# Router products taken in front of the norm, rows turned inside the output projection, one weight block requested earlier

## The chip, the cores and the metric

The kernel runs on one core of a Trainium2 chip. The time is that of the device for one execution, in microseconds (us); lower is better. The core has TensorE (PE, matrix products into PSUM), VectorE (DVE), ScalarE (ACT), GpSimd (POOL), SyncE (SP, which issues most transfers here) and 16 DMA engines.

## The reference

One decoder layer on 576 tokens (a prompt of 512 and 8 sequences of 8), 1024 wide: a mixer, then hierarchical mixture of experts.

```python
def _layer(x, ...):
    m, new_pool, new_conv = _mixer(x, ...)            # h = x @ w_in, pooling and short convolution, @ w_out
    x = _layer_norm(DEEPNORM_ALPHA * x + m, ln1_g, ln1_b)
    f = _hier_moe(x, w_group, b_group, w_expert, b_expert, w1, w3, w2)
    x = _layer_norm(DEEPNORM_ALPHA * x + f, ln2_g, ln2_b)

def _hier_moe(x, ...):
    g_logits = xf @ w_group + b_group                 # 4 groups, the best one is taken
    e_logits = xf @ w_expert + b_expert               # 8 experts in each, the best two of the group
    ...
    for e in range(N_EXPERTS):                        # 32 experts, 1024 -> 512 -> 1024
        hdn = jax.nn.silu(xf @ w1[e]) * (xf @ w3[e])
        acc = acc + combine[:, e:e + 1] * (hdn @ w2[e])
```

`_layer_norm` subtracts the row's mean, divides by the root of its variance plus 1e-5, multiplies by g and adds b.

## The kernel before, in words

Tokens are in five tiles, four of 128 rows and one of 64 (`ROWS`). The kernel has these stages:

1. Input projection. `project(c)` for 16 parts of w_in, each in three products of high and low parts (fp32r), 48 matrix products a part; pooling maps and the convolution run on DVE and ACT beside it.
2. Output projection. `out_project(h, j)` for the two halves h of the 1024 columns and the tiles j, 24 products each, from `mix_high`, `mix_low` and `wout_part`. In its second half DVE adds the residual, takes mean and variance (`deviation_of`), and normalises the row in place in `x_tok` (`norm1`). When a tile is normalised (`x1_ready`), PE turns it (`turn_x1`: eight transposes), ACT copies it to `x1T` and stores the rows to `x1_rows` in DRAM, and `route` multiplies the turned rows by the router's 36 columns. These pieces stand between the tiles' projections, one or two tiles behind.
3. Choice. DVE adds the bias (`keep_logits`), chooses group and experts in a chain of dependent small operations (`choose`), and PE counts positions from the mask. `keep_warm(n)` is n products of the identity with itself, whose results nobody reads.
4. Fetch. `fetch_first` picks the rows of the first expert tile out of `x_tok` with a one-hot product; `turn_first` turns them. The second tile's rows come by an indirect DMA from `x1_rows` (POOL) and are turned by `turn_second`.
5. Experts. 33 tiles of 64 slots; each has w1, w3 and w2, 2 MB each, streamed through ten blocks of SBUF (`EARLY_BLOCKS`). SP issues the loads in the fixed order of `LOADS`: w1 and w3 of tile 0, of tile 1, w2 of tile 0, and so on. One of the odd pairs after the first, seven in all, has its rows picked by PE (`pick_pair`), the others come by DMA. Load n from the eleventh on waits until the block that it replaces has been used (`block_free`). There are 96 loads.

The first ten blocks share their memory with the stages before, so each has its own condition: load 9 after the first value weights, loads 1 and 2 after the input projection, 5 after the mixer's tails are stored, 6 and 7 after the first half of the output projection, and 0, 3, 4 and 8 after the second half (`out_done` at 10). `mix_high` lies across blocks 3 and 4.

All engines run in order, each its own queue; semaphores join them.

## Time and profile before

| | us |
|---|---|
| three timed runs, median (lowest to highest) | 699.1 (696.45 to 699.15) |
| the profiled execution, its own time | 694.83 |
| its span | 693.1 |
| PE busy in it | 649.9 (94%) |
| DVE busy | 316.2 (46%) |
| ACT busy | 226.1 (33%) |
| POOL busy | 151.5 (22%) |

The mean granted clock was 0.992 of full speed. The span runs from the first to the last instruction; the execution's own time has 1.7 us more. Busy shares are means over stages with different limits, so what a change is worth is read from the stage in which it acts, and from what waits there last.

### The profile page before, as it was taken

To read this page: it belongs to the slowest core of one execution; us is meant where nothing else is said; L and a number is where in the kernel's file an instruction comes from. 1 tells how busy PE (TensorE), PEld (TensorE's weight loads), DVE (VectorE), ACT (ScalarE), POOL (GpSimd) and SP (SyncE) were. 2 spreads that over 40 slices of the span, in tenths; PEclk is the share of its full clock that TensorE was granted. 3 is DMA by queue.
4 is the path that set the end of the run, shared out by engine and by line. 5 is a ranking of instruction groups with operands and counts; after the bars stand their busy time and mean duration, and the time that the engine had idled before them with its cause. 6 is when DMAs were issued, how large, how long until landed. Compare 5 with 4: busy or idle time off the path is not lost.

```text
span 693.1 us, 10915 instructions
## 1 busy us (share of the span) xinstructions
PE 649.9 (94%) x4334; PEld 424.7 (61%) x4334; DVE 316.2 (46%) x829; ACT 226.1 (33%) x330; POOL 151.5 (22%) x180
## 2 busy tenths in 40 slices
PE   5999999999989999999999999999999799789883
PEld 5899999878866555554555555455454454445451
DVE  3562485716676416155154345335433425332555
ACT  3423313301122323344344145253344233413331
POOL 1000000000001214233233323313413223231433
PEclk9999999999999999999999999999999999999998
DMA  9892231836296999999999999999999999999991
GB/s 259 268 320 74 80 122 35 335 133 258 72 425 274 361 389 417 421 417 420 417 418 414 418 417 420 421 422 419 419 419 421 417 418 420 418 421 417 421 402 60
DMA packets 44781, 233.89 MB, mean 337 GB/s; under 512 B 13231, under 2 KB 17839, under 8 KB 27881
## 3 DMA queue, kind: packets, MB, share of 16 engines
q1 hardware_dynamic: 32191, 220.92, 79.0%
q0 software_dynamic: 11680, 9.58, 4.3%
q10 hardware_dynamic: 857, 2.67, 1.0%
q8 instruction: 35, 0.57, 0.3%
q14 instruction: 18, 0.14, 0.1%
HBM read 234.55 MB, written 30.20 MB: 382 GB/s over the span
## 4 chain that ended last, share of the span: by engine, by line
PE 73%; DMA 13%; SPq 7%; DVE 4%; issue 1%; ACT 1%; POOL 0%; DVEq 0%; POOLq 0%; ACTq 0%
PE ps L736 24%; PE ps L546 14%; PE ps L757 12%; DMA blocks<-in_w 12%; PE ps L708 8%; PE ps L603 7%; SPq L403 4%; SPq L407 2%; PE ps L722 2%; PE ps L745 1%; DMA blocks<-in_w_in 1%; PE ps L632 1%; PE ps L679 1%; PE ps L616 1%; DVE blocks L1309 1%
## 5 line engine op out<-in xcount | busy, mean ns | idle before, releaser
L736 PE MATMUL ps<-blocks,ln 128*64 128x256 f32 x2112 | 241.2, 381 | 14.1 <-DMA blocks<-in_w 12.7
L736 PEld LDWEIGHTS ps<-blocks,ln 128*64 128x64 f32 x2112 | 151.7, 137 | 101.8 <-issue 33.4
L757 PE MATMUL ps<-blocks,hT 128*64 128x512 f32 x528 | 120.2, 597 | 6.3 <-DMA blocks<-in_w 4.1
L757 PEld LDWEIGHTS ps<-blocks,hT 128*64 128x64 f32 x528 | 37.2, 137 | 68.0 <-issue 57.3
L1033 ACT ACTIVATE std<-rstd,eps 128x1 f32<-128x1 f32 x32 | 9.4, 294 | 167.6 <-DVEq L1612 167.5
L708 PE MATMUL ps<-x_tok,hot 128*128 128x512 f32 x140 | 62.0, 597 | 0.0
L1152 POOL DMA_INDIRECT out<-prev,final_row x32 | 32.2, 1006 | 97.6 <-DVE prev L1618 97.6
L1148 POOL DMA_INDIRECT prev<-first_outputs,final_row x32 | 33.5, 1048 | 80.8 <-DMA first_outputs<-ye,first_row 48.4
L983 ACT ACT_TABLE_LOAD x30 | 38.5, 1283 | 29.9 <-PE ps L736 29.5
L708 PEld LDWEIGHTS ps<-x_tok,hot 128*128 128x128 f32 x140 | 26.0, 190 | 35.8 <-issue 35.8
L1580 DVE SCALAR_TENSOR_TENSOR h_rows<-silu,slot_gate,ps 128x256 f32<-128x256 f32 x33 | 15.8, 480 | 67.8 <-PE ps L736 67.7
L546 PE MATMUL ps<-xT_high,w_in_high 128*128 128x288 f32 x256 | 41.1, 303 | 3.6 <-ACT w_in_high L842 2.4
L1585 DVE COPY hT<-ps 128x256 f32<-128x256 f32 x33 | 13.9, 420 | 61.8 <-PE ps L745 61.7
L546 PE MATMUL ps<-xT_low,w_in_high 128*128 128x288 f32 x256 | 40.0, 299 | 0.0
L546 PE MATMUL ps<-xT_high,w_in_low 128*128 128x288 f32 x256 | 39.1, 295 | 0.0
L546 PEld LDWEIGHTS ps<-xT_high,w_in_high 128*128 128x128 f32 x256 | 36.4, 191 | 4.4 <-ACT w_in_high L842 2.6
L1033 ACT ACT_TABLE_LOAD x30 | 38.5, 1283 | 0.5
L1591 DVE TENSOR_TENSOR ye_more<-ye_more,ps 128x512 f32<-128x512 f32 x16 | 11.0, 687 | 59.2 <-PE ps L757 59.2
L1591 DVE TENSOR_TENSOR ye<-ye,ps 128x512 f32<-128x512 f32 x16 | 11.0, 688 | 56.3 <-PE ps L757 56.3
L1144 POOL DMA_INDIRECT first_outputs<-ye,first_row x16 | 17.7, 1105 | 87.0 <-DVE ye L1591 86.3
L546 PEld LDWEIGHTS ps<-xT_low,w_in_high 128*128 128x128 f32 x256 | 36.6, 192 | 0.0
L842 ACT ACTIVATE ln<-ps 128x512 f32<-128x512 f32 (+1 forms) x36 | 18.7, 571 | 52.6 <-PE ps L722 47.6
(246 smaller groups left out, 803.9 us busy)
## 6 DMA issues: line engine op xcount, KB each, us to landing
blocks<-in_w SPq DMA_DIRECT2D x94, 2048.0 KB, 27.9
blocks<-in_w_in SPq DMA_DIRECT2D x3, 2048.0 KB, 10.3
blocks<-in_w_out SPq DMA_DIRECT2D x2, 2048.0 KB, 7.7
blocks<-in_w SPq DMA_DIRECT2D x4, 1024.0 KB, 38.6
x_tok<-in_x_prompt SPq DMA_DIRECT2D x4, 512.0 KB, 5.1
blocks<-in_w_in SPq DMA_DIRECT2D x4, 512.0 KB, 11.4
first_outputs<-in_x_prompt SPq DMA_DIRECT2D x4, 512.0 KB, 8.7
x_rows<-x_tok ACTq DMA_DIRECT2D x4, 512.0 KB, 2.8
```

The costliest lines, as they stand in the source:

```text
L403: sp.dma_start(in_block(b), src.rearrange("(p c) f -> p c f", c=KD)).then_inc(block_loaded[b], 16)
L546: mm = pe.matmul(ps[:, 2 * (c % 2) + h, 0:HALF], w_part[a][:, c % 2, k, :], xT[b][:, k, h * HALF:(h + 1) * HALF], start=(i == 0 and k == 0 ...
L603: mm = pe.matmul(ps[0:r, o % 4, :], mix_part[a][:, k, j * P:j * P + r], wout_part[h][b][:, k, :], start=(i == 0 and k == 0), stop=(i == 2 ...
L708: mm = pe.matmul(ps[:, BX[g], :], hot[:, j, :], x_tok[:, j, g * DH:(g + 1) * DH], start=(j == 0), stop=(j == NT - 1))
L736: mm = pe.matmul(ps[64 * g:64 * g + 64, bank, 0:FH], x, w[:, k, g * FH:(g + 1) * FH], start=(k == 0), stop=(k == KD - 1))
L757: mm = pe.matmul(ps[64 * g:64 * g + 64, BY, :], hT[:, k % 2, k // 2 * SLOTS:(k // 2 + 1) * SLOTS], w[:, k, g * DH:(g + 1) * DH], start=(k ...
L842: return nc.scalar.activation(out, in_, ACT.Copy, **kw)
L983: nc.scalar.activation(silu, ps[:, B1, 0:FH], ACT.Silu).then_inc(silu_ready, 1)
L1033: nc.scalar.activation(std[:, :], rstd[:, 1, 1:2], ACT.Sqrt, bias=eps[:, 1:2]).then_inc(std_ready, 1)
L1148: return g.indirect_dma_start(out=prev[w], out_offset=None, in_=first_rows[:, :], in_offset=rows_at(idx), bounds_check=last_row, oob_is_er ...
L1152: return g.indirect_dma_start(out=prompt_rows[:, :], out_offset=rows_at(idx), in_=prev[w], in_offset=None, bounds_check=last_prompt_row, o ...
L1591: v.tensor_tensor(ye[u], ye[u], ps[:, BY, :], ALU.add).then_inc(y_kept, 1)
```

## The change

The router's product is taken of the rows in front of the norm. With row x, mean m, root r = 1 / sqrt(variance + eps), router weights W and norm parameters g, b, the logits are r * (x @ (g*W)) - r * m * sum(g*W) + sum(b*W) + bias. So:

- DVE scales the router's weights by g, multiplies them by b into `router_b`, and sums both over the columns' k in four operations between `low_of_w(8)` and `low_of_w(9)`; one product with a stationary of ones (`ones_wide`, filled by POOL) sums them over the partitions between `project(8)` and `project(9)`. Three small DVE operations take the results behind the first half of the output projection. g and b come in four more small loads (`ln1_cols`), and the router's weights in a new order of rows.
- `turn_x1(j, h)` turns half a tile, four transposes, and waits for the residual only; the two halves stand inside the next tile's `out_project`, ahead of its k = 2 and k = 3, and the last tile's first half ahead of k = 6 of its own. `route(j)` follows the projection of tile j + 1. `x1T` has two buffers.
- DVE takes the first half's statistics in the first half of the projection, the second's behind the second residual (`measure`). It normalises the rows once they are turned (`normalise`), except the last tile's, which POOL normalises in three operations. `keep_logits` is two dependent operations for one. `fetch_first` waits for all rows.
- The fifteen warming products behind the last `route` become six groups of three, each behind three more steps of DVE.
- `mix_high` is moved into block 4 (its last part behind `mix_low`), and load 3 is issued with loads 1 and 2.

```diff
@@ SP
-            sp.dma_start(w_router[:, :, 0:EG], w_group.rearrange("(p k) c -> p k c", k=KD)).then_inc(router_loaded, 16)
-            sp.dma_start(w_router[:, :, EG:NR], w_expert.rearrange("(p k) c -> p k c", k=KD)).then_inc(router_loaded, 16)
+            for h in range(2):
+                half = slice(h * DH, (h + 1) * DH)
+                for w, c in ((w_group, slice(0, EG)), (w_expert, slice(EG, NR))):
+                    sp.dma_start(w_router[:, h * KH:(h + 1) * KH, c],
+                                 w[half, :].rearrange("(q i) c -> q i c", i=KH)).then_inc(router_loaded, 16)
+                for a, x in enumerate((ln1_g, ln1_b)):
+                    sp.dma_start(ln1_cols[:, a, h * KH:(h + 1) * KH],
+                                 x[half].rearrange("(q i) -> q i", i=KH)).then_inc(router_loaded, 16)
...
             load(1)
             load(2)
+            load(3)
...
             sp.wait_ge(out_done, 2 * NT)
             load(0)
-            load(3)
             load(4)
             load(8)
@@ PE
-            for c in range(6, 13):
+            for c in range(6, 9):
+                project(c)
+            pe.wait_ge(router_scaled, 1)
+            pe.wait_ge(ones_made, 1)
+            pe.wait_ge(map_kept, NG)
+            pe.matmul(ps[:, 7, 0:2 * NR], ones_wide, router_sums, start=True, stop=True).then_inc(router_summed, 1)
+            for c in range(9, 13):
                 project(c)
...
                     if o == 0:
                         pe.wait_ge(mix_is_low, k + 1)
+                    for at_k, turn in between:
+                        if at_k == k:
+                            turn()
...
-            def turn_x1(j):
+            def turn_x1(j, h):
+
                 r = ROWS[j]
-                pe.wait_ge(x1_ready, j + 1)
+                pe.wait_ge(out_kept, h * NT + j + 1)
                 if j:
-                    pe.wait_ge(x1T_ready, 2 * j)
+                    pe.wait_ge(x1T_ready, 2 * j + h - 1)
                 else:
                     pe.wait_ge(tail_kept, 2)
...
-            out_project(1, 1)
-            turn_x1(0)
-            for j in range(2, NT):
-                out_project(1, j)
-                route(j - 2)
-                turn_x1(j - 1)
+            for j in range(1, NT):
+                turns = [(2, lambda: turn_x1(j - 1, 0)), (3, lambda: turn_x1(j - 1, 1))]
+                if j == NT - 1:
+                    turns.append((6, lambda: turn_x1(j, 0)))
+                out_project(1, j, turns)
+                route(j - 1)
+            turn_x1(NT - 1, 1)
             pe.wait_ge(out_kept, NT + 3)
             keep_warm(4)
-            route(NT - 2)
-            turn_x1(NT - 1)
-            keep_warm(2)
             route(NT - 1)
 
-
-            keep_warm(15)
+            for i in range(1, 7):
+                pe.wait_ge(step, ROUTE_STEP + 3 * i)
+                keep_warm(3)
...
                 pe.wait_ge(hot_ready, 1)
+                pe.wait_ge(x1_ready, NT)
@@ ACT
+            for j in range(NT - 1):
+                deviation(j)
                 keep_x1T(j)
+                if j:
+                    store_x1(j - 1)
+            keep_x1T(NT - 1)
+            deviation(NT - 1)
+            store_x1(NT - 2)
+            store_x1(NT - 1)
@@ POOL
+            r, row = ROWS[NT - 1], x_tok[0:ROWS[NT - 1], NT - 1, :]
+            pool.wait_ge(rows_scaled, 1)
+            pool.wait_ge(x1_turned, 2 * NT)
+            g.tensor_scalar(row, row, mv1[0:r, NT - 1, 0:1], rstd[0:r, NT - 1, 0:1],
+                            ALU.subtract, ALU.mult).then_inc(rows_centred, 1)
+            pool.wait_ge(rows_centred, 1)
+            g.tensor_tensor(row, row, ln1[0:r, 0, :], ALU.mult).then_inc(rows_centred, 1)
+            pool.wait_ge(rows_centred, 2)
+            g.tensor_tensor(row, row, ln1[0:r, 1, :], ALU.add).then_inc(x1_ready, 1)
             pool.wait_ge(second_row_ready, 2)
             pool.wait_ge(x1_stored, 16 * NT)
@@ DVE
+            def measure(j):
+
                 r = ROWS[j]
                 settled(residual(1, j))
                 dve.sem_inc(out_kept, 1)
+                settled(v.bn_stats(stats1[0:r, j, 6:12], x_tok[0:r, j, DH:D]))
+                settled(v.bn_aggr(mv1[0:r, j, :], stats1[0:r, j, :]))
+                dve.sem_inc(var_ready, 1)
...
             def keep_logits(j):
+
                 r = ROWS[j]
                 dve.wait_ge(logits_done, j + 1)
-                v.tensor_tensor(logits[0:r, j, :], ps[0:r, 6 + j % 2, 0:NR], b_router[0:r, :], ALU.add).then_inc(logits_kept, 1)
...
+                settled(v.scalar_tensor_tensor(logits[0:r, j, :], router_sums[0:r, 0:NR], mv1[0:r, j, 0:1],
+                                               ps[0:r, 6 + j % 2, 0:NR], ALU.mult, ALU.add))
+                v.scalar_tensor_tensor(logits[0:r, j, :], logits[0:r, j, :], rstd[0:r, j, 0:1], b_router[0:r, :],
+                                       ALU.mult, ALU.add).then_inc(logits_kept, 1)
...
+            for j in range(NT - 1):
+                measure(j)
+                scale_of(j)
+                if j:
+                    keep_logits(j - 1)
+                normalise(j)
+            measure(NT - 1)
+            keep_logits(NT - 2)
+            scale_of(NT - 1)
+            dve.sem_inc(rows_scaled, 1)
+            keep_logits(NT - 1)
             dve.wait_ge(logits_kept, NT)
```

PE's queue around the turning of tile 0 (`ident` is the identity of a transpose, `mix_high` and `mix_low` the projection's rows). Before, at the end of `out_project(1, 1)` and the start of `out_project(1, 2)`:

```order
L603 MATMUL ps<-w_out_high_58,mix_low 128x512
L616 MATMUL ps<-ident,x_tok 128x128 [waits tail_kept,x1_ready]
L616 MATMUL ps<-ident,x_tok 128x128 x7
L603 MATMUL ps<-w_out_high_58,mix_high 128x512 [waits out_kept]
L603 MATMUL ps<-w_out_low_59,mix_high 128x512
```

After, at k = 1 to 3 of `out_project(1, 1)`:

```order
L641 MATMUL ps<-w_out_high_59,mix_low 128x512
L656 MATMUL ps<-ident,x_tok 128x128 [waits tail_kept,out_kept]
L656 MATMUL ps<-ident,x_tok 128x128 x3
L641 MATMUL ps<-w_out_high_59,mix_high 128x512
L641 MATMUL ps<-w_out_low_60,mix_high 128x512
L641 MATMUL ps<-w_out_high_59,mix_low 128x512
L656 MATMUL ps<-ident,x_tok 128x128 [waits tail_kept,out_kept]
L656 MATMUL ps<-ident,x_tok 128x128 x3
```

The transposes have moved forward by most of a projection, into it, and wait for the residual (`out_kept`) and not for the normalised row (`x1_ready`).

PE's queue from the last but one router product to the mask (`ye` holds the router's weights, `io` and `x1T` the turned rows). Before:

```order
L632 MATMUL ps<-ye,io 128x36 [waits logits_kept,x1T_ready]
L632 MATMUL ps<-ye,io 128x36 x7
L616 MATMUL ps<-ident,x_tok 128x64 [waits x1T_ready,x1_ready]
L616 MATMUL ps<-ident,x_tok 128x64 x7
L624 MATMUL ps<-ident 128x128 x2
L632 MATMUL ps<-ye,io 64x36 [waits logits_kept,x1T_ready]
L632 MATMUL ps<-ye,io 64x36 x7
L624 MATMUL ps<-ident 128x128 x15
L661 MATMUL ps<-io,before 128x32 [waits mask_ready]
```

After:

```order
L656 MATMUL ps<-ident,x_tok 128x64 [waits x1T_ready,out_kept]
L656 MATMUL ps<-ident,x_tok 128x64 x3
L662 MATMUL ps<-ident 128x128 [waits out_kept]
L662 MATMUL ps<-ident 128x128 x3
L670 MATMUL ps<-ye,x1T 64x36 [waits logits_kept,x1T_ready]
L670 MATMUL ps<-ye,x1T 64x36 x7
L662 MATMUL ps<-ident 128x128 [waits step]
L662 MATMUL ps<-ident 128x128 x2
```

Of the last two rows there are six pairs. Only half a tile of 64 rows is turned behind the projections now, one wait for a copy is left where there were two, and the warming products wait for DVE's steps.

POOL's queue ahead of the gather of the second tile's rows (`equal` holds the means). Before:

```order
L1136 COPY io<-blocks 128x2 [waits in_dve]
L1137 COPY io<-blocks 128x16
L1166 DMA ln_78<-x_rows,second_row 128x1024 [waits x1_stored,second_row_ready]
L1194 MEMSET xe_odd 128x1024 [waits table_done]
L1166 DMA xe_odd<-x_rows,pair_row 128x1024 [waits xe_turned,y_filled,pairs_ready,prev_cleared]
```

After:

```order
L1183 COPY io<-blocks 128x16
L1239 TENSOR_SCALAR x_tok<-x_tok,equal,rstd 64x1024 [waits x1_turned,rows_scaled]
L1242 TENSOR_TENSOR x_tok<-x_tok,ln_80 64x1024 [waits rows_centred]
L1244 TENSOR_TENSOR x_tok<-x_tok,ln_80 64x1024 [waits rows_centred]
L1212 DMA ln_80<-x_rows,second_row 128x1024 [waits x1_stored,second_row_ready]
```

Three operations stand ahead of the gather, and the last of them releases PE's fetch and ACT's store of the last tile.

## Rows read from the trace of the kernel before

**Rows 1.** which waits of TensorE for weights there are: engine, line, cause, us, times, longest

```profile
PE ps L736 <- DMA blocks<-in_w: 12.7, 9, 2.5
```

**Rows 2.** chain that ended last, in order of time: start, us, what

```profile
619.35 40.15 DMA blocks<-in_w
...
659.64 3.67 PE ps L736 x32
```

**Rows 3.** stretches: length, busy PE, PEld, DVE, ACT, POOL, then clock, DMA share, GB/s

```profile
216.00:218.00 2.00, 2.00 (x22) 1.34 (x20) 1.90 (x9) 0.39 (x1) 0.00 (x0) 1.00 0.27 41
...
260.00:508.00 248.00, 248.00 (x1622) 131.74 (x1620) 106.35 (x317) 95.23 (x131) 78.87 (x77) 1.00 1.01 419
```

**Rows 4.** timeline of SP's DMA queue: start us, us

```profile
127.37 27.22 SPq L403 DMA_DIRECT2D blocks<-in_w  x3
...
188.42 0.38 SPq L400 DMA_DIRECT2D blocks<-in_w  x1
...
216.65 0.37 SPq L407 DMA_DIRECT2D blocks<-in_w  x1
```

**Rows 5.** timeline of TensorE, 165 to 220 us

```profile
165.39 1.16 PE L616 MATMUL ps<-ident,x_tok 128*128 128x128 f32 x8 [0.28 <-DVE x_tok L1402]
...
166.31 0.47 PE L603 MATMUL ps<-w_out_high,mix_high 128*128 128x512 f32 x1
...
171.88 1.87 PE L632 MATMUL ps<-ye,io 128*128 128x36 f32 x16
...
174.45 0.48 PE L603 MATMUL ps<-w_out_high,mix_high 128*128 128x512 f32 x1
...
192.42 1.98 PE L632 MATMUL ps<-ye,io 128*128 128x36 f32 x16 [0.48 <-ACT io L842]
...
195.35 0.71 PE L624 MATMUL ps<-ident 128*128 128x128 f32 x4
...
195.99 1.12 PE L632 MATMUL ps<-ye,io 128*64 128x36 f32 x16
...
197.04 3.62 PE L624 MATMUL ps<-ident 128*128 128x128 f32 x30
...
202.44 0.19 PE L661 MATMUL ps<-io,before 128*128 128x32 bf16 x1 [1.78 <-DVE io L1448]
...
204.25 3.34 PE L679 MATMUL ps<-x_tok,hot_first 128*64 128x512 f32 x8
...
207.98 2.77 PE L679 MATMUL ps<-x_tok,hot_first 128*64 128x512 f32 x11
...
212.93 7.13 PE L736 MATMUL ps<-blocks,ln 128*64 128x256 f32 x64 [0.75 <-ACT ln L842]
...
219.99 1.16 PE L697 MATMUL ps<-ident,ln 128*128 128x128 f32 x8
```

**Rows 6.** timeline of VectorE, 197 to 219 us

```profile
197.37 0.17 DVE L1428 TENSOR_REDUCE io<-logits 128x5 f32<-128x20 f32 x1
...
203.70 0.89 DVE L1475 TENSOR_TENSOR hot_first<-slots,first_slot 128x320 f32<-128x320 bf16 x2
...
218.53 0.41 DVE L1547 TENSOR_TENSOR io<-io,gates 128x255 f32<-128x255 f32 x1
```

**Rows 7.** one stretch as in rows 3, by granted clock

```profile
204.00:205.00 1.00, 0.96 (x3) 0.30 (x4) 1.00 (x3) 0.00 (x0) 0.00 (x0) 0.50 1.00 426
```

**Rows 8.** one period of the projections, columns as in rows 3

```profile
174.00:182.00 8.00, 8.00 (x49) 7.02 (x48) 4.67 (x8) 1.38 (x3) 0.00 (x0) 1.00 0.17 68
```

**Rows 9.** timeline of GpSimd, its copies and one fill

```profile
24.69 0.19 POOL L1129 COPY io<-blocks 128x15 f32<-128x15 f32 x1 [20.89 <-ACT blocks L842]
...
29.06 0.29 POOL L1131 COPY io<-blocks 128x120 f32<-128x120 f32 x1 [4.17 <-DVE blocks L1320]
...
223.99 0.95 POOL L1194 MEMSET xe_odd<- 128x1024 f32 x1 [14.18 <-PE ps L812]
```

**Rows 10.** tensor x_rows: from issue to landing of its transfers

```profile
DMA to landing us min/median/max: 2.7/10.5/13.7
```

More of the change, by code:

```diff
@@ L44 @@
 PAIRS = E // 2
+ROUTE_STEP = 74
 EARLY_BLOCKS = 10
@@ L164, in build @@
         ln1 = sb("ln1", [P, 2, D])
+        x1T_more = nc.alloc_sbuf_tensor_at("x1T_more", [P, 4 * P], F32, offset=small[0])[:, :]
         h_rows = sb("h_rows", [P, FH])[:, :]
@@ L217, in build @@
         mixT = io_flat[:, 0:2 * NG * T].rearrange("p (j t) -> p j t", j=2 * NG)
-        x1T = io_flat[:, NT * D:NT * D + D].rearrange("p (k t) -> p k t", k=KD)
+        x1T_of = [[x.rearrange("p (k t) -> p k t", k=4) for x in pair] for pair in
+                  ((x1T[:, 0:4 * P], x1T[:, 4 * P:8 * P]),
+                   (ye_flat[:, 0:4 * P], x1T_more))]
         here = 2 * NG * T
@@ L588, in _, with out_project @@
                 project(c)
-            def out_project(h, j):
+            def out_project(h, j, between=()):
                 o = h * NT + j
@@ L606, in out_project @@
                 mm.then_inc(out_done, 1)
-            def turn_x1(j):
+            def turn_x1(j, h):
                 r = ROWS[j]
-                pe.wait_ge(x1_ready, j + 1)
+                pe.wait_ge(out_kept, h * NT + j + 1)
                 if j:
-                    pe.wait_ge(x1T_ready, 2 * j)
+                    pe.wait_ge(x1T_ready, 2 * j + h - 1)
                 else:
                     pe.wait_ge(tail_kept, 2)
-                for k in range(KD):
-                    mm = pe.transpose(ps[:, 4 + k // 4, (k % 4) * r:(k % 4 + 1) * r], x_view[0:r, j, k, :],
-                                      ident[0:r, 0:r])
-                    if k % 4 == 3:
-                        mm.then_inc(x1_turned, 1)
+                rows = x_tok[0:r, j, h * DH:(h + 1) * DH].rearrange("p (q i) -> p i q", i=KH)
+                for i in range(KH):
+                    mm = pe.transpose(ps[:, 4 + h, i * r:(i + 1) * r], rows[:, i, :], ident[0:r, 0:r])
+                mm.then_inc(x1_turned, 1)
             def keep_warm(products):
@@ L924, in high_of_mix @@
                     act.wait_ge(in_dve, k + 1)
-                copy(mix_high[:, k, :], mixT[:, k, :]).then_inc(mix_is_high, 1)
+                copy(mix_part(0, k), mixT[:, k, :]).then_inc(mix_is_high, 1)
             def high_of_wout(h):
@@ L1254, in _ @@
             steps = [0]
-            deviations = [0]
             def settled(ins):
@@ L1334, in _ @@
                 low_of_w(c)
+            dve.wait_ge(router_loaded, 160)
+            dve.wait_ge(map_done, NG)
+            g_cols, b_cols = [ln1_cols[:, a, :].unsqueeze(2).to_broadcast([P, KD, NR]) for a in range(2)]
+            settled(v.tensor_tensor(router_b, w_router, b_cols, ALU.mult))
+            settled(v.tensor_reduce(router_sums[:, NR:2 * NR], router_b.rearrange("p k c -> p c k"), AX.X, ALU.add))
+            settled(v.tensor_tensor(w_router, w_router, g_cols, ALU.mult))
+            v.tensor_reduce(router_sums[:, 0:NR], w_router.rearrange("p k c -> p c k"), AX.X,
+                            ALU.add).then_inc(router_scaled, 1)
             for c in range(NG):
@@ L1397, in norm1, with scale_of, normalise @@
                 dve.sem_inc(out_kept, 1)
+                settled(v.bn_stats(stats1[0:r, j, 6:12], x_tok[0:r, j, DH:D]))
+                settled(v.bn_aggr(mv1[0:r, j, :], stats1[0:r, j, :]))
+                dve.sem_inc(var_ready, 1)
+            def scale_of(j):
+                dve.wait_ge(std_ready, j + 1)
+                settled(v.reciprocal(rstd[0:ROWS[j], j, 0:1], std[0:ROWS[j], :]))
+            def normalise(j):
+                r = ROWS[j]
                 row = x_tok[0:r, j, :]
-                deviation_of(row, r)
-                v.scalar_tensor_tensor(row, row, mv[0:r, 0:1], ln1[0:r, 0, :], ALU.subtract, ALU.mult)
-                scale_of(r, rstd[0:r, j, 0:1])
+                dve.wait_ge(x1_turned, 2 * j + 2)
+                settled(v.scalar_tensor_tensor(row, row, mv1[0:r, j, 0:1], ln1[0:r, 0, :], ALU.subtract, ALU.mult))
                 v.scalar_tensor_tensor(row, row, rstd[0:r, j, 0:1], ln1[0:r, 1, :], ALU.mult,
```

81 lines of the change are left out of this document (42 added, 39 removed).

## The prediction

> **What bounds the kernel now.** The waits for weights come first [rows 1]: in the expert stage TensorE (PE) waits for weight blocks nine times, 12.7 us in all, on this line alone, so it is not PE that sets the end there. The chain of waits says what does [rows 2]: its last long piece ahead of the last experts is a DMA of 40.15 us, whose landing releases the products at 659.64. The stretches show that this is a stream without holes [rows 3]: DMA share 0.27 at 216 to 218 us, but 1.01 over the 248 us from 260 on, at 419 GB/s. The time is therefore the start of that stream, plus a fixed number of bytes at a fixed rate, plus a tail that the change doesn't touch. What starts it is on SP's queue [rows 4]: the eleventh block is issued at 216.65, when the first tile's first product (w1, begun at 212.93 [rows 5]) has freed its block. Blocks that land before that moment bring nothing by themselves: the stream's 86 loads, from the eleventh to the ninety-sixth, come after it either way. So the question is how much earlier the first tile starts, and behind that how PE gets from the second half of the output projection through router, choice of experts and fetch of the first rows to 212.93.
>
> **PE from the projection to the last logits.** Prices by starts [rows 5]: eight transposes 0.92 (165.39 to 166.31), one projection of 24 products 5.57 (to 171.88), one tile's router products with the next transposes 2.57 (to 174.45), so the router's eight alone 1.65. The change does the same number of each. It takes out two waits, 0.28 for the normalised rows of tile 0 and 0.48 for the copy ahead of the fourth router product, and two warming products, 0.64 (195.35 to 195.99). It removes the pipeline's emptying around these waits too: the rest of PE's time between the pieces, of which I take 0.2. Sum: 1.6 us off the end of the last router product, 197.1 before. The turns no longer wait for VectorE (DVE) to normalise, only for the residual. DVE was busy 4.67 of 8 us in one tile's period [rows 8]; it loses one of two statistics there (done earlier, in the first half, where it waits for PE) and gains one small operation on the logits, so it keeps up.
>
> Added ahead of it, between two input projections, is one product with a 128 x 128 stationary of ones. Eight router products of that kind take 1.65, so one is 0.2, on the path since PE never rests there. Its four DVE operations on 128 x 288 values lie in DVE's idle time in front of the ninth weight part, and the router's loads were needed only at 155 us before and are 50 us early still; nothing.
>
> **The choice.** DVE begins it at 197.37 [rows 6]. It now does two dependent operations per tile on the logits instead of one: 0.25 more behind the last product (one such operation with its wait, by the pitch of the neighbours). Then PE warms up in six groups of three, each behind three of DVE's steps. The fifteen warming products of before are 30 instructions in 3.62 [rows 5], 0.24 a product, so a group is 0.7, just the pace of DVE's three steps; the sixth group starts behind the eighteenth step, some 0.5 ahead of the mask, and so ends about 0.2 after it. That is 0.2 later for the positions. So the positions come 1.6 - 0.2 - 0.25 - 0.2 = 0.95 us earlier than at 202.44.
>
> **The clock.** This is the second half of the gain. Before, PE stood idle 1.78 us ahead of 202.44 [rows 5], and the granted clock was then 0.50, the 1.2 GHz level, at 204 to 205 us [rows 7]. The fetch of the first rows felt it: its first eight instructions took 3.34, its last eleven 2.77 [rows 5], 0.24 each by the first and last start and the small ones between; at that pace eight take 1.9, so the slow clock cost 1.4. With the warming spread up to the mask, the 1.78 us hole is gone and PE is never quiet for over about half a microsecond. I take it that the clock stays at 2.4 GHz: 1.4 us. The Trainium skill says likewise (TensorE: Matmul & The Clock Gate, section Loop structure matters more than you think) that products behind a long wait run cold; by that rule, the trace agrees.
>
> **Rows of the last tile on GpSimd.** They are normalised there by three operations on 64 x 1024, and the fetch now waits for them. The trace has no such operation. Lower bound: three fills of 1024 at 0.95 [rows 9], 2.9. The copies give 0.19 for 15 elements and 0.29 for 120: a slope of 0.95 ns an element, so 1.1 for one input; with twice that for two inputs 1.1 + 2 x 2.1 = 5.3, which I take. Upper bound: the 120-element copy whole, 2.4 ns an element, 2.5 + 2 x 5.0 = 12.5. They can start at about 194.9: the last turn ends some 2 us before the last router product (195.4 after the change), then copy, square root and reciprocal. So they end at 200.2 (197.8 to 207.4). The first one-hot was there at 204.15 [rows 6] and will be at 203.2, so 3 us of cover remain. The skill's GPSIMD Engine Reference, section Elementwise — side-by-side cycle accounting, has 2.6 cycles an element at 1.2 GHz for two inputs: an estimate of 2.2 us each, by which the sum stays as it is.
>
> The store of these rows leaves 7 us later than at 193.6. Stores took 2.7 to 13.7 to land [rows 10]; with 10.5 it is at 211, the gather behind it needs some 6 more, and it is wanted at 218: covered. Loads: three blocks instead of four are left for the end of the projection, which comes at about 191.1 and not 188.4 [rows 4] since the turns are now inside it. Three at 5 us each land by 206.5, ahead of the first tile. The fourth goes out with the group at 127.37 [rows 4], into time in which DMA has room. Zero on both sides.
>
> **Sum.** The first tile's product and with it the stream's first load: 0.95 + 1.4 = 2.35 earlier. The next step is not free: the turn of the second tile's rows, 219.99 before, waits for DVE's table too, whose last operation started at 218.53 [rows 6] and ended at 218.94, so only 1.05 us of reserve; DVE comes 0.95 earlier, and the turn at 218.05, 1.95 earlier. The later loads follow this. The stream's start moves by 1.95 to 2.35; I take 2.1. All of it goes through to the end, because PE has spare time up to there. The profiled execution took 694.8 (span 693.1 and 1.7 around it): 692.7. The three timed runs have their median at 699.1, 4.3 above it: 697.0.
>
> **Rivals.**
> - *The clock falls all the same.* The 1.4 is then missing: 0.95 for the stream, 698.1. For it: groups of 0.7 us with the fetch held until 203.2 still leave small holes. Against: before, it fell only behind the one long hole. 0.15.
> - *More is gained.* The timed runs lie 1.7 to 4.3 above the profiled one, and nothing in the profile says where. If part is a second slow stretch at this place (another 1.4) or more waiting between DVE and PE, the change takes that too: 3.5 to 5 us, 694.9. 0.20.
> - *GpSimd is late.* If its three operations take 12.5, the rows come at 207.4, 4.2 after the one-hot: the fetch starts that much later, the stream 1.9 later than before, 701.0. It cancels the gain from 10.7 us on, and from 14.2 on the kernel is over 0.5% slower. For it: 64 rows use only part of that engine, perhaps no faster than 128. Against: its copies' slope. 0.12.
> - *DVE is slowed beside GpSimd.* From 195.8 to 200.2 both read two tensors from the same memory. If DVE's choice, 4.4 us of such small operations, takes half as long again, the positions come 1.25 later than before and the clock's 1.4 just pays it: 699.0. No row of this trace has the two side by side. The skill has the rule (GPSIMD Engine Reference, section Specifications): the memory interfaces are shared, with contention for VectorE operations with two inputs. 0.08.
> - *The stream doesn't start earlier in effect.* Between 218 and 246 us other transfers run, and a hole there could swallow what comes first: 699.1. Against: a tile's three blocks need 15 us at 419 GB/s, and PE uses them faster while it has them, so requests pile up. 0.05.
>
> **Numbers.** My forecast has 0.40: 697.0, its own range 695.5 to 698.5. The range for all is 693.7 to 700.5: it takes in the larger gain, the two cases near no change and half of GpSimd's, and the runs' own scatter of 2.7. About 0.5%, 3.5 us, is what a measurement of this kernel tells from none. Faster by more: most of the second rival and the forecast's lower edge, 0.26. Slower by more: GpSimd beyond its bound, and a scatter upwards, 0.10. Within: 0.64.
>
> **What would show it.** Right: router's last product about 195.4; granted clock 1.00 from 200 to 210; the fetch's twenty instructions within 5.3 us; GpSimd's three done by 201; w1 of the first tile at about 210.6; eleventh load at 214.3; DMA share again 1.01 to the end and the last w3's product about 657.5. Wrong: a wait of PE at the fetch released by GpSimd, a clock of 0.50 there, DVE's steps between logits and mask longer than 0.23 each, or PE waiting at the second turn for the gather. The forecast fails most easily at the GpSimd price, which no row has, and at the clock.

## The result and the profile after

| | before | changed |
|---|---|---|
| timed runs, median (lowest to highest), 20 each | 695.96 (691.34 to 702.71) | 699.22 (696.24 to 704.16) |
| ratio of the changed to before, 95% interval | | 1.0059 (1.0032 to 1.0086) |
| profiled execution: own time, span | 694.83, 693.1 | 699.03, 697.3 |

The change made the kernel slower by 0.59%, where 0.3% faster was forecast. That 699.2 lies inside the forecast range, 693.7 to 700.5, is luck: the first three runs of the kernel before, whose median was the base of the sum, were high, 699.1 against 695.96 over twenty, and from 695.96 the same range would have ended at 697.4. (The ratios and intervals leave the few disturbed runs out.) A ratio can lie up to 0.3% from the quotient of the two medians, about 2 us, so a difference of that size should not be read from either alone.

One thing must be taken out before two executions are compared. The input projection ended at a different moment in each: load 1, which SP issues at its end, is this row of SP's queue in the kernel before.

```profile
126.96 0.37 SPq L400 DMA_DIRECT2D blocks<-in_w  x1
```

The same timeline of the changed kernel has load 1 at 125.99, and the eleventh load at 219.93:

```profile
125.99 0.37 SPq L428 DMA_DIRECT2D blocks<-in_w  x1
...
219.93 0.37 SPq L435 DMA_DIRECT2D blocks<-in_w  x1
```

Over the eleven profiled executions without tests ahead of it, it lies between 124.8 and 127.5. So I count from it. The eleventh load, which starts the stream, came 3.28 us later than in [rows 4], and counted from load 1 4.25 later. Now VectorE from the last tile's logits to the mask:

```profile
195.39 0.25 DVE L1471 SCALAR_TENSOR_TENSOR logits<-logits,rstd,ye 64x36 f32<-64x36 f32 x1
195.67 0.17 DVE L1501 TENSOR_REDUCE io<-logits 128x5 f32<-128x20 f32 x1
195.88 0.18 DVE L1502 TENSOR_TENSOR io<-logits,io 128x20 f32<-128x20 f32 x1
...
197.57 0.20 DVE L1501 TENSOR_REDUCE io<-io 128x5 f32<-128x40 f32 x1
197.80 2.35 DVE L1502 TENSOR_TENSOR io<-io 128x40 f32<-128x40 f32 x1
200.18 2.38 DVE L1503 TENSOR_TENSOR io<-io,rev 128x40 f32<-128x40 f32 x1
202.59 0.20 DVE L1504 TENSOR_REDUCE io<-io 128x5 f32<-128x40 f32 x1
...
203.52 0.20 DVE L1502 TENSOR_TENSOR io<-io 128x40 f32<-128x40 f32 x1
```

Two operations of 40 elements took 2.35 and 2.38 us; the same line takes 0.20 six microseconds later. GpSimd's timeline has what lay beside them:

```profile
193.89 3.78 POOL L1239 TENSOR_SCALAR x_tok<-x_tok,equal,rstd 64x1024 f32<-64x1024 f32 x1 [92.56 <-DVEq L1493]
197.75 2.33 POOL L1242 TENSOR_TENSOR x_tok<-x_tok,ln 64x1024 f32<-64x1024 f32 x1
200.16 2.33 POOL L1244 TENSOR_TENSOR x_tok<-x_tok,ln 64x1024 f32<-64x1024 f32 x1
```

GpSimd's second operation ends at 200.08 and VectorE's at 200.15; the third at 202.49, VectorE's at 202.56. Each two-input VectorE operation that began while one of GpSimd's two-input operations ran ended with it, while the two-input ones of the choice beside GpSimd's first, all in its last 1.8 us, took 0.18 to 0.33. In TensorE's timeline the warming groups, which count VectorE's steps, come late too:

```profile
193.95 1.12 PE L670 MATMUL ps<-ye,x1T 128*64 128x36 f32 x16
196.33 1.72 PE L662 MATMUL ps<-ident 128*128 128x128 f32 x12 [1.26 <-DVE io L1503]
200.20 0.94 PE L662 MATMUL ps<-ident 128*128 128x128 f32 x6 [2.15 <-DVE io L1502]
203.08 4.21 PE L662 MATMUL ps<-ident 128*128 128x128 f32 x18 [1.94 <-DVE io L1505]
207.08 0.23 PE L697 MATMUL ps<-io,before 128*128 128x32 bf16 x1
...
208.94 1.94 PE L716 MATMUL ps<-x_tok,hot_first 128*64 128x512 f32 x8
...
216.22 7.13 PE L773 MATMUL ps<-blocks,ln 128*64 128x256 f32 x64 [0.75 <-ACT ln L879]
```

And these stretches have the granted clock, in the same columns as [rows 3]:

```profile
200.00:202.00 2.00, 0.94 (x6) 0.74 (x6) 1.97 (x2) 0.00 (x0) 1.92 (x2) 0.93 1.02 430
202.00:204.00 2.00, 0.92 (x4) 0.92 (x5) 1.76 (x8) 0.93 (x1) 0.50 (x1) 0.50 1.02 434
...
206.00:208.00 2.00, 2.00 (x27) 1.83 (x25) 0.08 (x1) 0.00 (x0) 0.00 (x0) 0.50 0.99 422
208.00:210.00 2.00, 2.00 (x12) 1.26 (x13) 1.90 (x7) 0.00 (x0) 0.00 (x0) 0.86 0.75 315
```

PE stood for 2.15 and 1.94 us, the clock was at its 1.2 GHz level from 202 to 208, and the last eighteen warming instructions took 4.21 instead of 2.2 (eighteen at the pace of the thirty in 3.62 of [rows 5]). The mask was ready at about 205.05, but the positions' products stand behind the warming and began at 207.08. The clock was back for the fetch: 1.94 for its first eight instructions, 3.34 in [rows 5].

The account, against [rows 4 to 6], each from load 1's issue:

| piece | before | changed | |
|---|---|---|---|
| load 1 to the start of the choice | 70.41 | 69.68 | -0.73 |
| choice to the positions' first product | 5.07 | 11.41 | +6.34 = 4.33 (VectorE held) + 2.01 (warming) |
| positions to the first w1 product | 10.49 | 9.14 | -1.35 |
| sum: load 1 to the first w1 product | 85.97 | 90.23 | +4.26 |

From that product to the last instruction it was 480.2 and 481.1 us: the rest of the kernel passes the start on. That last part varies by itself, from 479.4 to 484.3 us over the eleven executions, and no run shows why. So below I read a variant's effect from where this first w1 product starts in its trace, and its time from the medians and ratios of many runs.

### The profile page after: what moved, and what is told of

Its sections match the earlier page's. It is cut to its first block, busy times and chain, and to the rows that moved or that the text cites. A ratio compares the mean times of both kernels' runs of the same rounds, so it can differ in the third digit from the quotient of the medians.

```text
span 697.3 us, 10961 instructions
## 1 busy us (share of the span) xinstructions
PE 650.8 (93%) x4338; PEld 426.6 (61%) x4338; DVE 323.3 (46%) x838; ACT 226.3 (32%) x330; POOL 161.4 (23%) x184
## 4 chain that ended last, share of the span: by engine, by line
PE 72%; DMA 18%; DVE 5%; SPq 3%; issue 1%; ACT 0%; POOL 0%; POOLq 0%; DVEq 0%
PE ps L773 24%; DMA blocks<-in_w 18%; PE ps L574 13%; PE ps L794 12%; PE ps L745 9%; PE ps L641 8%; PE ps L759 2%; SPq L395 1%; PE ps L782 1%; PE ps L670 1%; PE ps L662 1%; DMA ye<-in_w_pool_map 1%; PE ps L656 1%; SPq L431 1%; DVE blocks L1363 1%
## 5 line engine op out<-in xcount | busy, mean ns | idle before, releaser
L574 PEld LDWEIGHTS ps<-xT_high,w_in_low 128*128 128x128 f32 x256 | 35.7, 188 | 0.0
```

What stands on the lines that cost most here:

```text
L574: mm = pe.matmul(ps[:, 2 * (c % 2) + h, 0:HALF], w_part[a][:, c % 2, k, :], xT[b][:, k, h * HALF:(h + 1) * HALF], start=(i == 0 and k == 0 ...
```

## The experiments

"w1" is the first w1 product's start counted from load 1's issue, in each kernel's profiled execution. The kernel before was timed again beside each group: its median was 696.70 beside one_input to before_two_input, 695.12 beside split to before_one_input, and 696.19 beside in_psum and one_input_again.

| kernel | median | ratio to before (95%) | w1 |
|---|---|---|---|
| before | | 1 | 85.97 |
| changed | 699.22 | 1.0059 (1.0032 to 1.0086) | 90.23 |
| one_input | 692.91 | 0.9965 (0.9933 to 0.9996) | 83.98 |
| on_vector | 694.91 | 1.0007 (0.9975 to 1.0039) | 85.12 |
| warm_at_once | 700.04 | 1.0052 (1.0017 to 1.0087) | 89.80 |
| before_two_input | 701.86 | 1.0102 (1.0065 to 1.0138) | 89.6 |
| split | 693.46 | 0.9989 (0.9966 to 1.0012) | 85.10 |
| split_warm_at_once | 696.02 | 1.0021 (0.9995 to 1.0046) | 87.53 |
| before_one_input | 697.43 | 1.0026 (0.9999 to 1.0054) | 85.41 |
| in_psum | 693.71 | 0.9962 (0.9940 to 0.9984) | 84.44 |
| one_input_again | 694.34 | 0.9962 (0.9933 to 0.9991) | 83.97 |

**Without GpSimd's two-input operations (one_input).** In the changed kernel:

```diff
-            pool.wait_ge(rows_centred, 1)
-            g.tensor_tensor(row, row, ln1[0:r, 0, :], ALU.mult).then_inc(rows_centred, 1)
-            pool.wait_ge(rows_centred, 2)
-            g.tensor_tensor(row, row, ln1[0:r, 1, :], ALU.add).then_inc(x1_ready, 1)
```

> The changed kernel without GpSimd's two two-input operations (scale by g, add b) on the last tile of 64 rows: that tile is only centred and divided, so this part of the computation is left out. In the changed kernel the first w1 product starts at 216.2. Theory 1 (GpSimd's two-input operations hold VectorE's): no VectorE operation between logits and mask takes over 0.5 us, the mask comes 4.3 earlier, the clock stays full and PE isn't behind the mask with its warming: w1 at 209.9, 6.3 earlier, the time some 3 us below the kernel before (ratio 0.996). Theory 2 (the spread warming itself makes the positions late): the positions stay 2 us behind the mask, w1 at about 212 or later. Theory 3 (the loss is in the reordered turns and waits): w1 stays near 216.

Measured: 0.9965, w1 83.98, that is 6.25 earlier than in the changed kernel. The last tile is left without gain and shift here, so the kernel does less than the reference. The two operations account for the whole loss, and what is left is a gain of 1.99 at w1.

**The rows on VectorE (on_vector).** GpSimd's three operations go; VectorE normalises the last tile ahead of its logits, and the warming counts from one step later:

```diff
-            dve.sem_inc(rows_scaled, 1)
+            normalise(NT - 1)
             keep_logits(NT - 1)
```

> The last tile is normalised on VectorE, ahead of its last logits, and GpSimd does nothing there. Two operations of 1.28; VectorE has 1.4 us of waiting at that place. Theory 1: 1.3 us are left on the path in place of 4.3 held plus 2.0 at the warming: w1 at 211.2, time some 1.7 us below the kernel before (ratio 0.9975). Theory 2: w1 at 213 or later, since the spread warming is kept. Theory 3: w1 near 217.5, 1.3 later than the changed kernel.

Measured: 1.0007, w1 85.12. VectorE's second operation, 1.28 us at 195.08, stands on the path and costs 1.14 of the 1.99. The first product came where it was expected; that it is still 0.85 earlier than before doesn't show in the ratio, whose interval allows for it.

**Warming in one piece (warm_at_once).** In the changed kernel:

```diff
-            for i in range(1, 7):
-                pe.wait_ge(step, ROUTE_STEP + 3 * i)
-                keep_warm(3)
+            keep_warm(15)
```

> The changed kernel with its fifteen warming products in one piece again, as before the change. Theory 1: VectorE's two operations are still 2.35 each, so the mask stays at 205; positions follow at once at 205.1, 2 us sooner than 207.1, but PE stands idle from 198.6 to 205.1, the clock is at 0.50 for the fetch, which then takes up to 8.3 and not 5.1: w1 between 214.2 and 217.4. Theory 2: the fifteen in a piece cure the loss, w1 at 213 or earlier, as before the change.

Measured: 1.0052, w1 89.80. VectorE's timeline has the same two long operations, 1.24 us later, as the input projection ended that much later here:

```profile
199.04 2.36 DVE L1500 TENSOR_TENSOR io<-io 128x40 f32<-128x40 f32 x1
201.43 2.38 DVE L1501 TENSOR_TENSOR io<-io,rev 128x40 f32<-128x40 f32 x1
```

So the spread warming doesn't cause the hold. Beside it, it neither pays nor costs much: it delays the positions by 2.0 and gives the fetch its clock back (first eight instructions 3.23 here, 1.94 in the changed kernel), and w1 differs by 0.43.

**The suspect alone, in the kernel before (before_two_input).** GpSimd, which had nothing to do there, adds two tensors four times beside the choice; VectorE waits for the last of them only behind its tables, long after they are done:

```diff
+            pool.wait_ge(logits_kept, NT)
+            for i in range(4):
+                if i:
+                    pool.wait_ge(spare_made, i)
+                g.tensor_tensor(spare[0:64, :], x_tok[0:64, 0, 0:DP], x_tok[0:64, 1, 0:DP], ALU.add).then_inc(spare_made, 1)
```

> The kernel before, and beside VectorE's choice four GpSimd additions of two tensors, 64 x 512 each, whose sum nobody reads. Theory 1: each takes about 1.2 and holds VectorE's next two-input operation to its end; about 4 us later to the mask, and the clock falls for longer: w1 at 217 to 219 instead of 212.9, time 4 to 6 us above the kernel before. Theories 2 and 3: VectorE's operations keep their 0.2 and w1 stays at 213.

Measured: 1.0102. GpSimd's first additions began at 196.36 and 197.69 (1.26 and 1.30 us), and VectorE's timeline reads:

```profile
196.30 0.17 DVE L1435 TENSOR_REDUCE io<-logits 128x5 f32<-128x20 f32 x1
196.51 1.14 DVE L1436 TENSOR_TENSOR io<-logits,io 128x20 f32<-128x20 f32 x1
197.69 0.18 DVE L1437 TENSOR_TENSOR io<-io,rev 128x20 f32<-128x20 f32 x1
197.90 0.18 DVE L1438 TENSOR_REDUCE io<-io 128x5 f32<-128x20 f32 x1
198.11 0.92 DVE L1439 TENSOR_TENSOR io<-io 128x20 f32<-128x20 f32 x1
```

GpSimd's end at 197.62 and 198.99, VectorE's at 197.65 and 199.03. The reductions, of one input, pass at 0.18. An operation of VectorE that begins at the same moment as GpSimd's can pass too, as the one at 197.69 did, and one of 0.33 at 199.07; there it was GpSimd's third addition, begun at 199.07, that took longer, 1.44. Four operations are held by 3.04 together, where about 4 was expected, and choice to positions takes 8.12 instead of 5.07. At w1 the loss is 3.65, but 1.0102 is some 7 us (the medians differ by 5.2): this execution was also 3.7 longer behind w1, and what is lost there stays open. None of the changed kernel's other edits is needed for VectorE to be held.

**One-input operations in that place (before_one_input).** The same with `g.tensor_scalar(spare[0:64, :], x_tok[0:64, 0, 0:DP], 2.0, 1.0, ALU.mult, ALU.add)`.

> As the kernel before with four GpSimd additions, but each with one tensor and constants (64 x 512). GpSimd takes longer for such an operation (3.8 us for 1024 elements in the changed kernel, 2.3 for two tensors). Theory 1, narrow: VectorE's choice keeps its pace, positions at 74.9 to 75.5 after load 1 as before, w1 at 86.0, time as before. If any long GpSimd operation held VectorE: the mask 6 us later.

Measured: 1.0026 (0.9999 to 1.0054), small and not certain. The expectation, that only GpSimd's two-input operations hold, was wrong, and its guess that a one-input operation takes longer was too. A GpSimd operation with one input holds VectorE as well, but takes only half as long: 0.61 from 196.31 and 0.61 from 198.58, in these rows of VectorE:

```profile
196.46 0.48 DVE L1436 TENSOR_TENSOR io<-logits,io 128x20 f32<-128x20 f32 x1
...
198.75 0.49 DVE L1436 TENSOR_TENSOR io<-io 128x40 f32<-128x40 f32 x1
```

They end at 196.94 and 199.24, GpSimd's at 196.92 and 199.19. Three operations are held by 0.67 together, exactly what the positions lose (5.74 instead of 5.07). The clock was at full speed for the fetch in this execution and gave 1.4 back, which is why its w1 is 85.41: the slow stretch lay earlier here (0.77 at 198 to 200 us), and the thirty warming instructions took 5.03 instead of 3.62.

**Which operations meet (side_by_side, side_by_side_more).** In the kernel before, in front of the third value weight, chains of dependent VectorE operations of 128 x 128, six or eight, each chain beside one GpSimd operation of 128 x 384 (one execution each, read from the trace only):

```diff
+            for i, kind in enumerate(("two", "one", "psum", "copy", "two", "two")):
+                dve.sem_inc(go, 1)
+                for k in range(6):
...
+                    if kind == "two":
+                        ins = v.tensor_tensor(out, a, b, ALU.add)
+                    elif kind == "one":
+                        ins = v.tensor_scalar(out, a, 2.0, 1.0, ALU.mult, ALU.add)
+                    elif kind == "psum":
+                        ins = v.tensor_tensor(out, a, ps[:, 7, 0:P], ALU.add)
```

> The kernel before with a small test in a stretch in which VectorE and GpSimd have nothing to do (70 to 80 us): six times one GpSimd operation of 384 elements beside a chain of six VectorE operations of 128 elements, each waiting for the one ahead. GpSimd: two tensors added four times, then scalars on one tensor, then a copy. VectorE: two tensors in SBUF; one tensor and constants; one tensor in SBUF and one in PSUM; a copy; and for GpSimd's last two kinds two tensors in SBUF. Theory 1 in its narrow form (both must have two SBUF inputs): one VectorE operation of the first chain is stretched to about GpSimd's 0.9, and none in the other five. In its wide form (GpSimd's two-input operation shuts VectorE out of SBUF altogether): one is stretched in each of the first four chains. If only the amount of memory traffic counted: all are a little slower, none stands out.

> The kernel before with five more short tests at the place of the first six, each a chain of eight dependent VectorE operations of 128 x 128 beside one GpSimd operation of 128 x 384: VectorE additions of two SBUF operands (0.29 us alone) beside GpSimd's tensor_scalar with scalars read per partition (the form that takes 3.78 us for 1024 elements in the changed kernel, so about 1.4 here), beside its tensor_scalar with constants, beside its fill, then VectorE's reduction and its scalar_tensor_tensor, each beside GpSimd's two-input addition (1.02 us). Theory (a VectorE operation that needs the second read path waits for any GpSimd operation that reads SBUF, and for no other): beside constants the one that meets it is held to GpSimd's end, at most 0.6 us, beside the fill none is, the reduction isn't held, scalar_tensor_tensor is held to about 1.1; beside the scalars per partition one is held to 1.4 us if that form keeps the path for its whole span. Rival for that form: in the changed kernel five operations of two SBUF operands ran at 0.18 to 0.33 inside its 3.78 us, so it doesn't keep the path for its whole span, and here none is held beyond 0.6.

The trace answers by line, with the shortest, median and longest duration of one in ns; the first test's lines are VectorE's additions of two SBUF operands (three chains), constants, additions with a PSUM operand, copies:

```profile
L1356 DVE TENSOR_TENSOR spare<-x_tok x18: 291/292/1104, 70.9 to 85.3; 128x128 f32<-128x128 f32 x18
L1358 DVE TENSOR_SCALAR spare<-x_tok x6: 227/228/1080, 73.8 to 76.0; 128x128 f32<-128x128 f32 x6
L1360 DVE TENSOR_TENSOR spare<-x_tok,ps x6: 286/286/290, 76.4 to 78.0; 128x128 f32<-128x128 f32 x6
L1362 DVE COPY spare<-x_tok x6: 226/228/1084, 78.5 to 80.6; 128x128 f32<-128x128 f32 x6
```

Beside GpSimd's addition one VectorE operation in each chain is held to 1.08 to 1.10, save in the chain that reads PSUM. Neither expected form fits, for VectorE's operations with constants and its copies are held, and those with a PSUM operand not; VectorE's additions are held beside GpSimd's tensor_scalar with constants (to 0.48) and beside its copy (to 0.62) too. GpSimd's additions took 1.02, but the first took 1.98, and the timelines show that it is held as well:

```profile
69.77 1.23 DVE L1290 TENSOR_TENSOR w_in_low<-blocks,w_in_high 128x1024 fp32r<-128x1024 f32 x1 [6.01 <-ACT w_in_high L846]
69.89 1.98 POOL L1141 TENSOR_TENSOR spare<-x_tok 128x384 f32<-128x384 f32 x1 [16.37 <-DVEq L1352]
70.91 1.10 DVE L1356 TENSOR_TENSOR spare<-x_tok 128x128 f32<-128x128 f32 x1
```

It began inside a VectorE operation of two SBUF operands and took 0.96 longer; VectorE's next then waited for it. In the second test, a scalar_tensor_tensor is held (1.14), a reduction never (0.28 to 0.29), nothing beside GpSimd's fill (0.29). Beside tensor_scalar with constants (0.66) one operation took 0.47. The form with scalars per partition took 2.73, and one of the five additions begun inside it 0.56, the others 0.28 to 0.29. This 2.73 is no price of the form, since it too began inside a VectorE operation of two SBUF operands:

```profile
68.17 1.23 DVE L1293 TENSOR_TENSOR w_in_low<-blocks,w_in_high 128x1024 fp32r<-128x1024 f32 x1 [6.01 <-ACT w_in_high L846]
68.31 2.73 POOL L1147 TENSOR_SCALAR spare<-x_tok 128x384 f32<-128x384 f32 x1 [16.41 <-DVEq L1355]
```

So that form holds VectorE for part of its span at most. In the changed kernel nobody was held beside its 3.78 us, but VectorE had no operation of two SBUF operands in its first 1.5 us; whether the form would hold one there stays open.

**VectorE does the work in its waits (split, split_warm_at_once).** GpSimd's three operations are taken out; VectorE does the first half in its wait for the last logits, the second behind the choice, and `store_x1(NT - 1)` goes behind ACT's exponentials:

```diff
+            last_rows = x_tok[0:ROWS[NT - 1], NT - 1, :]
+            dve.wait_ge(x1_turned, 2 * NT)
+            settled(v.scalar_tensor_tensor(last_rows, last_rows, mv1[0:ROWS[NT - 1], NT - 1, 0:1],
+                                           ln1[0:ROWS[NT - 1], 0, :], ALU.subtract, ALU.mult))
             keep_logits(NT - 1)
...
+            v.scalar_tensor_tensor(last_rows, last_rows, rstd[0:ROWS[NT - 1], NT - 1, 0:1],
+                                   ln1[0:ROWS[NT - 1], 1, :], ALU.mult, ALU.add).then_inc(x1_ready, 1)
```

> The changed kernel with the last tile normalised on VectorE in two pieces: the first operation in the wait for the last logits, the second in the wait for the positions; ScalarE stores the tile after its exponentials. Measured from the issue of load 1 (end of the input projection) the first w1 product starts at 86.0 in the kernel before, 90.2 in the changed one, 85.1 with both operations ahead of the logits. Theory 1: each wait hides most of its operation, 0.6 are left: 84.6, the time 2 to 2.5 us below the kernel before (ratio 0.9965). If the second operation or the late store stops the fetch or the second tile's rows: 85.5 or later, ratio 0.999 or more.

> The split kernel with the fifteen warming products in one piece. The one point that differs is the clock: as in the kernel before, PE stands idle nearly 2 us ahead of the mask, the granted clock is 0.50 over part of the fetch, which takes 1.4 longer; the positions come 0.2 sooner. So w1 at 85.8 from load 1, 1.2 later than split. If the spread warming has no worth where nothing holds VectorE: w1 at 84.4.

Measured: 0.9989 and 1.0021, w1 85.10 and 87.53; 0.9965 and 84.6 were expected of split. The wait for the positions was no free place. PE's first position product came at 199.84 in split, its fetch at 202.67, 2.83 later, against 1.77 in one_input_again (201.67 to 203.44); VectorE's timeline has its second operation right ahead of the slots:

```profile
200.46 1.28 DVE L1526 SCALAR_TENSOR_TENSOR x_tok<-x_tok,rstd,ln 64x1024 f32<-64x1024 f32 x1
201.66 0.22 DVE L1540 SCALAR_TENSOR_TENSOR first_slot<-ps,io 128x5 f32<-128x5 f32 x2
```

The pair shows what the spread warming is worth without a hold. In one piece, PE stood 2.19 us ahead of the positions, the clock was 0.50 from 204 to 208, the fetch's first eight instructions took 3.68, and w1 came 2.43 later, twice the 1.2 expected; the spread one kept 1.00 throughout, and the eight took 1.94. The timed medians lie 2.56 apart.

**The hold taken away with all the work kept (in_psum).** The changed kernel, its choice with one operand of every two-input operation in PSUM:

```diff
+        kept = [ps[:, 7, 256 + 40 * i:256 + 40 * (i + 1)] for i in range(5)]
+        g_hot, g_tmp = [a[:, 0:20].rearrange("p (n e) -> p n e", n=NT) for a in kept[0:2]]
+        e_tmp, e_val, e_second = [a.rearrange("p (n e) -> p n e", n=NT) for a in kept[2:5]]
+        gmax, m2_again = ps[:, 7, 460:465], ps[:, 7, 465:470]
```

> The changed kernel with the choice's intermediate tiles (g_hot, g_tmp, e_tmp, e_val, the group maximum and the second expert's mark) in a free part of a PSUM bank, so that each two-input operation of VectorE's choice reads one operand from PSUM and one from SBUF; two short operations are added behind the mask (a second reduction and a second comparison, about 0.4 us together on VectorE) because an operation can't read both operands from PSUM. GpSimd's three operations, its two two-input ones of 2.33 us among them, stay as they are. In the test side by side, six VectorE additions with one PSUM operand kept their 0.29 us beside a GpSimd addition of 1.01 us, and with two SBUF operands the first was held to 1.10. Theory (a VectorE operation of two SBUF operands waits for GpSimd's whole two-input operation, one with a PSUM operand doesn't): no operation of the choice takes over 0.45 us, the 4.3 us of the changed kernel are gone, warming and clock with them, the first w1 product starts about 84.4 us after load 1's issue (measured 90.2 in the changed kernel, 83.98 where GpSimd's two were left out), and the kernel gives one_input's time plus 0.4: ratio to before 0.9970 (0.994 to 1.000), faster than before and 5 us under the changed kernel. Rival (GpSimd slows VectorE whatever VectorE reads, or PSUM operands cost by themselves): w1 89 to 90 us after load 1, ratio 1.005.

> The changed kernel without GpSimd's two two-input operations again (the last tile is left without gain and shift, so its output isn't the reference's), on the chip and beside the runs of in_psum. Theory: ratio 0.9965 (0.993 to 1.000) as before, and in_psum within 1 us above it. Rival (its first ratio was scatter): 1.000, as for the version that has VectorE do the work.

Measured: 0.9962, w1 84.44 (84.4 expected). GpSimd's timeline, then VectorE's beside it:

```profile
198.60 2.34 POOL L1245 TENSOR_TENSOR x_tok<-x_tok,ln 64x1024 f32<-64x1024 f32 x1
201.02 2.35 POOL L1247 TENSOR_TENSOR x_tok<-x_tok,ln 64x1024 f32<-64x1024 f32 x1
```

```profile
198.68 0.21 DVE L1505 TENSOR_TENSOR ps<-ps,io 128x40 f32<-128x40 f32 x1
198.92 0.21 DVE L1506 TENSOR_TENSOR ps<-ps,rev 128x40 f32<-128x40 f32 x1
...
201.29 0.32 DVE L1524 TENSOR_TENSOR io<-ps,io 128x160 bf16<-128x160 f32 x1
```

The same operations beside the same GpSimd work: 0.21 instead of 2.35. All the work is kept, and the kernel beats both: 0.38% under before and, by the two ratios to before (it wasn't timed beside the changed kernel), some 1% under the changed one. Its interval and that of one_input_again, timed beside it, are the same within 0.1%.

## Why the prediction was wrong

- **GpSimd at no cost: the step that failed.** "3 us of cover remain" was right as far as it went: the rows were ready at 202.49, long before the one-hots, and PE's fetch never waited for them. But the sum priced only the wait for GpSimd's result. What its operations do to VectorE while they run was a rival with 0.08 and the wrong shape: "half as long again" over the 4.4 us of the choice, +2.2. The runs show another rule: a VectorE operation of two SBUF operands that begins while GpSimd's runs waits for its end, whatever its own length. With two GpSimd operations of 2.33 that is 4.33. The prediction's own sign for it, steps of VectorE longer than 0.23 between logits and mask, is what came. A rival of that shape could have been priced from the rows: two operations priced at 2.1 each, each stopping a chain of 0.2 us steps for its length, give about 4.2.
- **It could have been read up.** The Trainium skill, SBUF — State Buffer, section Who interferes with whom, says that the ports which VectorE and GpSimd share are an exclusive lock, that VectorE with two SBUF inputs contends there with a GpSimd instruction that reads SBUF, that a reduction never contends, that copies and tensor_scalar can, and that one SBUF input at most doesn't otherwise. The traces agree in each point (2.35 and 2.38; 0.29; 1.08; 0.29 with PSUM); GpSimd's tensor_scalar with scalars per partition, whose 3.78 us held nobody and whose 2.73 us held one addition to 0.56, wasn't met over its whole span. I had weighed the shorter sentence of the Trainium skill's GPSIMD Engine Reference, section Specifications, and read "contention" as a slowdown.
- **The warming: right by itself, wrong beside a hold.** The last group cost 0.18 where nothing was held (choice to positions 5.25 in one_input, 5.07 before), 0.2 predicted. But a warming tied to VectorE's steps inherits VectorE's delays: PE stood, the clock fell, and eighteen instructions at half speed stood ahead of the positions, 2.0 us that the sum and the rival both left out.
- **The clock: right, with some luck in the execution.** 1.40 at the fetch, as forecast, in one_input, split, in_psum, and even in the changed kernel. But the kernel before doesn't always pay it: before_one_input and side_by_side keep its warming in one piece, and their fetch had its first eight instructions in 1.94, the slow stretch lying in the warming (5.03 and 5.06 instead of 3.62). How often the timed runs of the kernel before are of either kind no run shows.
- **PE from the projection to the logits: mis-sized.** 1.6 off the last router product was predicted, 1.07 measured from load 1's issue (69.03 to 67.96). The second operation on the logits cost 0.34, 0.25 predicted. Together 0.73 instead of 1.35; the difference is 0.6 of a gain of 2. The product with the stationary of ones lies ahead of load 1, so this count doesn't see its 0.2.
- **GpSimd's price: 3.3 too low, but no wait came of it.** 5.3 by the copies' slope, 8.6 measured with the steps between (3.78, 2.33, 2.33): the two-input ones 2.1 against 2.33, the one-input one 1.1 against 3.78. Within 2.9 to 12.5, and still hidden.
- **The gain reaches the end: right.** Without the hold the terms come to -1.07 + 0.34 + 0.18 - 1.40 = -1.95; w1 gave -1.99, and the medians of one_input, one_input_again and in_psum lie 3.8, 1.9 and 2.5 under before (2.4, 2.6 and 2.6 by the ratios), 2.1 forecast.

The forecast's mechanisms were thus right but for one, and that one was three times as large as all the others together. The chance of "slower", 0.10, came from a late result of GpSimd, not from its company.

## What to carry to other kernels

Before work is moved to an idle GpSimd, look at what VectorE does in that stretch: if it is a chain of small operations with two SBUF operands, or copies, that sets the end, each GpSimd operation that reads SBUF can cost the chain up to its whole length. One long GpSimd operation of two inputs is the worst neighbour of many short VectorE ones; move it in time, or give the VectorE operations one operand in PSUM, which cost two short extra operations here (w1 was 0.5 later than in one_input_again). And work that paces one engine by another's steps (a warming, here) arrives late just when the other engine does: ahead of something urgent it was worth 2.4 us where nothing was held, and nothing beside the hold.

## What the runs showed of the hardware that I had not expected

- A VectorE operation of 0.20 us took 2.35 and 2.38 beside GpSimd's additions and multiplications of 2.33, ending 0.02 to 0.07 after GpSimd's in every choice and at most 0.16 after it in the tests. It wasn't slowed but held.
- It goes both ways: GpSimd's addition of 1.02 us took 1.98 when it began inside a VectorE operation of two SBUF operands.
- One operand in PSUM removes it: 0.286 to 0.290 us in six of six, and 0.21 in the choice.
- GpSimd's tensor_scalar with scalars per partition is slower than its two-input operations: 3.78 against 2.33 us for 64 x 1024, in each of five executions. With constants it is faster: 0.66 against 1.01 for 128 x 384.
- 64 rows seem no cheaper on GpSimd than 128: its two-input operations took 1.01 us for 384 elements of 128 rows, 1.26 for 512 of 64 and 2.33 for 1024 of 64, all near one line of 2.0 to 2.1 ns an element.
